# Forgetting attention pairs: the high halves of weight strips and of the output projection's row tiles made by ScalarE instead of GpSimd

## What is computed

```
h = x @ w_in                                    # q, k, v of both head groups, and the forget gates
cum = cumsum(log_sigmoid(f_logit))              # per forgetting head
logits = q.k * scale + cum_q - cum_k            # causal
ob = softmax(logits) @ v                        # forgetting heads
mixer = concatenate([oa, ob]) @ w_o             # one output projection
x = layer_norm(ALPHA * x + mixer)
```

## Time and profile before

| | |
|---|---|
| median of three runs | 2824.18 us |
| the profiled execution | 2827.21 us, its span 2825.40 us |
| TensorE busy | 2687.5 us, 95% of the span |
| VectorE busy | 1903.7 us, 67% |
| ScalarE busy | 1080.0 us, 38% |
| GpSimd busy | 1676.1 us, 59% |
| granted TensorE clock | 0.993 of full speed |
| the four forgetting pairs | from 296 to 509 us |

### The profile page before, as it was taken

The page is one execution under the profiler, slowest core; times in us unless marked ns, Lnnn a source line. Parts: engine busy times, 40 slices in busy tenths (PEclk is TensorE's granted clock), DMA queues, the critical chain, the costliest instruction groups (busy, mean ns, idle before and its releaser), DMA issues.

```text
span 2825.4 us, 42474 instructions
## 1 busy us (share of the span) xinstructions
PE 2687.5 (95%) x15813; PEld 1363.5 (48%) x16096; DVE 1903.7 (67%) x2637; ACT 1080.0 (38%) x1665; POOL 1676.1 (59%) x916
## 2 busy tenths in 40 slices
PE   7999898899999999999899999899999999999998
PEld 4666554354444444444444444456654444444443
DVE  6788778575666674256999999688847656664043
ACT  3566566243333210014554343666643433331000
POOL 4777656336676679845347777711113666675884
PEclk9999999999999999999999999999999999999999
DMA  4122455631111253332213222488873111113332
GB/s 150 50 64 72 90 119 119 193 115 60 58 53 55 68 179 127 105 132 83 53 38 142 111 79 100 114 183 185 185 208 132 68 60 60 60 54 126 127 105 97
DMA packets 299309, 294.82 MB, mean 104 GB/s; under 512 B 239408, under 2 KB 239536, under 8 KB 299168
## 3 DMA queue, kind: packets, MB, share of 16 engines
q1 hardware_dynamic: 287360, 268.90, 33.1%
q10 hardware_dynamic: 11808, 23.99, 2.6%
HBM read 189.51 MB, written 35.70 MB: 80 GB/s over the span
## 4 chain that ended last, share of the span: by engine, by line
PE 78%; DVE 6%; issue 5%; ACT 4%; DMA 4%; POOL 2%; ACTq 1%; POOLq 0%; DVEq 0%; SPq 0%
PE ps L1691 23%; PE ps L334 20%; PE ps L316 14%; PE ps L650 4%; PE ps L2529 4%; PE ps L399 4%; DMA pt<-split 3%; PE ps L920 2%; PE ps L2019 2%; PE ps L656 1%; PE ps L2063 1%; DVE split L848 1%; PE ps L2557 1%; PE ps L891 1%; DVE prob L1035 1%
## 5 line engine op out<-in xcount | busy, mean ns | idle before, releaser
L273 POOL TENSOR_TENSOR w_hi<-w_stage,ones 128x1024 bf16<-128x1024 f32 (+1 forms) x115 | 238.5, 2074 | 138.1 <-PE ps L334 85.3
L276 POOL TENSOR_TENSOR w_lo<-w_stage,w_hi 128x1024 bf16<-128x1024 f32 (+1 forms) x115 | 265.2, 2306 | 9.0
L1508 DVE SCALAR_TENSOR_TENSOR x_res<-x_res,ps 128x1024 f32<-128x1024 f32 x32 | 39.0, 1218 | 319.6 <-PE ps L334 318.8
L334 PE MATMUL ps<-w_hi,hid_hi 128*128 128x512 bf16 x689 | 206.4, 379 | 1.6 <-POOL w_lo L276 0.8
L334 PE MATMUL ps<-w_hi,hid_lo 128*128 128x512 bf16 x690 | 206.5, 379 | 0.7
L334 PE MATMUL ps<-w_lo,hid_hi 128*128 128x512 bf16 x690 | 206.4, 379 | 0.7
L2529 PE MATMUL ps<-lat_hi,q_now 128*128 128x512 bf16 (+3 forms) x736 | 185.9, 326 | 7.6 <-DVE row_max L2616 6.8
L316 PE MATMUL ps<-xt_hi,w_hi 128*128 128x512 bf16 x598 | 179.2, 380 | 3.1 <-DVE score L2178 2.5
L316 PE MATMUL ps<-xt_hi,w_lo 128*128 128x512 bf16 x596 | 179.0, 380 | 0.8 <-issue 0.2
L316 PE MATMUL ps<-xt_lo,w_hi 128*128 128x512 bf16 x592 | 178.1, 380 | 0.8
L1691 PE MATMUL ps<-xt_lo,w_hi 128*128 128x512 bf16 x426 | 161.5, 379 | 0.5
(11 more groups left out here) (309 smaller groups left out, 7507.6 us busy)
## 6 DMA issues: line engine op xcount, KB each, us to landing
w_stage<-in_l_up SPq DMA_DIRECT2D x88, 512.0 KB, 3.8
w_stage<-in_l_down SPq DMA_DIRECT2D x88, 512.0 KB, 3.7
w_stage<-in_l_o SPq DMA_DIRECT2D x32, 512.0 KB, 6.2
w_stage<-in_l_q SPq DMA_DIRECT2D x32, 512.0 KB, 5.1
q_split<-q_out SPq DMA_DIRECT2D x32, 512.0 KB, 2.6
q_now<-q_split SPq DMA_DIRECT2D x16, 1024.0 KB, 5.7
w_stage<-in_l_qkv SPq DMA_DIRECT2D x24, 512.0 KB, 4.1
x_spilled<-x_res ACTq DMA_DIRECT2D x16, 512.0 KB, 2.6
```

Of the source, the lines that this page charges most:

```text
L273: pool.tensor_tensor(hi, w_stage[slot][:, 0:cols], ones[:, 0:1].to_broadcast([P, cols]), ALU.mult).then_inc(w_cast[slot], 1)
L276: pool.tensor_tensor(lo, w_stage[slot][:, 0:cols], hi, ALU.subtract).then_inc(w_split[slot], 1)
L334: mm = pe.matmul(ps[:, bank + h, :], a[:, k, rows], w[:, h * HALF:(h + 1) * HALF], start=(k == first and m == 0), stop=(k == tiles - 1 and ...
```

## The change

In the forgetting pairs, GpSimd no longer makes high halves of weights. ScalarE makes them with a copy that rounds to bfloat16, at the end of a slot, after the exponential: strips 2, 0 and 1 in slots 2, 6 and 11, the row tiles 3, 0, 1 in slots 7, 8 and 12 of pair 6, and the row tiles 2, 4, 5, 6, 7 in slots 3, 4, 6, 9 and 11 of pair 7. The waits for the load and for the last use of the buffer go with the copy to ScalarE. GpSimd waits for the copy and subtracts. Its steps for the tiles of pair 7 move from 1, 3, 5, 7, 9 to 3, 4, 6, 9, 11. ScalarE's loop over pairs 5 and 6 is written out, since its slots now differ. Loads, SyncE's list, TensorE's and VectorE's lists are the same.

```diff
@@ -989,6 +989,7 @@
                     act.activation(take[t % 4][:, 0:n], banks(2 * (t % 2))[:, 0:n], ACT.Exp, scale=SB_SCALE,
                                    bias=neg_max[:, t % 4:t % 4 + 1],
                                    accum_out=row_sum[:, t % 4:t % 4 + 1]).then_inc(s_sfree, 1)
+                    fox_weights_hi(act, pair, slot)
 
         def pair_vector(dve, pair, kind, prev, project):
 
@@ -1048,6 +1049,29 @@
             pool.wait_ge(w_cast[n], feed_qkv.use(n, pair) + 1)
             pool.tensor_tensor(w_lo[n][:, :], w_stage[n][:, :], w_hi[n][:, :], ALU.subtract).then_inc(w_split[n], 1)
 
+        def fox_weights_hi(act, pair, slot):
+
+            qkv = {2: (2, pair + 1), 6: (0, pair + 2), 11: (1, pair + 2)}
+            outputs = {7: 3, 8: 0, 12: 1} if pair == N_PAIRS - 2 else {3: 2, 4: 4, 6: 5, 9: 6, 11: 7}
+            if slot in qkv and qkv[slot][1] < N_PAIRS:
+                n, of = qkv[slot]
+                act.wait_ge(w_loaded[n], 16 * (feed_qkv.use(n, of) + 1))
+                act.wait_ge(s_pj, 6 * (of - 1) + 2 * (n + 1))
+                act.activation(w_hi[n][:, :], w_stage[n][:, :], ACT.Copy).then_inc(w_cast[n], 1)
+            elif pair >= N_PAIRS - 2 and slot in outputs:
+                n = outputs[slot]
+                act.wait_ge(w_loaded[feed_o0.slot(n)], 16 * (feed_o0.use(n, 0) + 1))
+                if n != 3:
+                    act.wait_ge(s_pj, 6 * (N_PAIRS - 1) + 2 * (n + 1) if n < 2 else 6 * N_PAIRS)
+                act.activation(held(feed_o0, n)[0], w_stage[feed_o0.slot(n)][:, 0:D_MODEL],
+                               ACT.Copy).then_inc(w_cast[feed_o0.slot(n)], 1)
+
+        def output_lo(pool, n):
+            slot = feed_o0.slot(n)
+            hi, lo = held(feed_o0, n)
+            pool.wait_ge(w_cast[slot], feed_o0.use(n, 0) + 1)
+            pool.tensor_tensor(lo, w_stage[slot][:, 0:D_MODEL], hi, ALU.subtract).then_inc(w_split[slot], 1)
+
         def pair_gpsimd_sb(pool, pair):
             for t in range(STEPS):
                 n = (query_block(t) + 1) * P
@@ -1177,36 +1201,22 @@
 
             def splits_ahead(pair):
                 def splits(t):
-                    if t == 2:
-                        split_qkv_hi(pool, 2, pair + 1)
-                    elif t == 3:
+                    if t == 3:
                         split_qkv_lo(pool, 2, pair + 1)
-                    elif t in (6, 11):
-                        split_qkv_hi(pool, t // 11, pair + 2)
                     elif t in (7, 12):
                         split_qkv_lo(pool, t // 12, pair + 2)
                 return splits
 
             def splits_last(t):
-                if t == 2:
-                    split_qkv_hi(pool, 2, N_PAIRS - 1)
-                elif t == 3:
+                if t == 3:
                     split_qkv_lo(pool, 2, N_PAIRS - 1)
-                elif t == 7:
-                    split_piece(pool, feed_o0, 3, 0)
-                elif t == 8:
-                    pool.wait_ge(s_pj, 6 * (N_PAIRS - 1) + 2)
-                    split_piece(pool, feed_o0, 0, 0)
-                elif t == 12:
-                    pool.wait_ge(s_pj, 6 * (N_PAIRS - 1) + 4)
-                    split_piece(pool, feed_o0, 1, 0)
+                elif t in (7, 8, 12):
+                    output_lo(pool, {7: 3, 8: 0, 12: 1}[t])
 
             def splits_o(t):
-                if t == 1:
-                    pool.wait_ge(s_pj, 6 * N_PAIRS)
-                ahead = {1: 2, 3: 4, 5: 5, 7: 6, 9: 7}
+                ahead = {3: 2, 4: 4, 6: 5, 9: 6, 11: 7}
                 if t in ahead:
-                    split_piece(pool, feed_o0, ahead[t], 0)
+                    output_lo(pool, ahead[t])
 
             with pool.Fori(N_SB // 2, N_PAIRS - 2) as pair:
                 pair_gpsimd_fox(pool, pair, splits_ahead(pair))
@@ -1231,7 +1241,16 @@
             make_current_qk(act, 1, 0)
             for hh in range(2):
                 make_current_v(act, hh, 0)
-            all_pairs(act, pair_scalar)
+            first_fox = N_SB // 2
+            pair_scalar(act, 0, "sb", None, True)
+            with act.Fori(1, first_fox - 1) as pair:
+                pair_scalar(act, pair, "sb", "sb", True)
+            pair_scalar(act, first_fox - 1, "sb", "sb", True)
+            pair_scalar(act, first_fox, "fox", "sb", True)
+            for pair in range(first_fox + 1, N_PAIRS - 1):
+                pair_scalar(act, pair, "fox", "fox", True)
+            pair_scalar(act, N_PAIRS - 1, "fox", "fox", False)
+            pair_scalar(act, N_PAIRS, None, "fox", False)
 
         def heads_vector(dve):
             for e in range(4, 6):
```

## The result

The changed kernel takes 2830.2 us (median of 19 runs, 2826.6 to 2832.6), the kernel before 2825.2 in the runs beside them (19 runs, 2823.1 to 2827.4). The ratio is 1.0015 with a 95% interval from 1.0009 to 1.0021: slower by 0.15%, some 4 us by the ratio and 5.0 between the medians, which is under the 0.2% taken as the bound. The forecast was +4.5 us.

What follows compares the result with a forecast made beforehand. The loop of VectorE and ScalarE was taken to set the pace in the last forgetting pair, with some TensorE slack in middle pairs. Terms 0.3 + 1.0 + 0.3 - 1.25 + 4.15 = +4.5 us gave median 2828.7, range 2819 to 2837.

Steps and rivals of the forecast that it cites:

- pair 4: New block at slot 2 costs 0.2, slots 5 to 7 end 0.2 early, slot 11 is 0.5 late: +0.3 after rounding.
- pair 5: Blocked or delayed splits around slots 2, 5 to 7 and 11 make the pair 1.0 us longer.
- pair 6: First, tile 3's passes given back at slot 7: -0.7; second, tile 1's copy in slot 12 delays a high half: +1.0.
- pair 7, first half: Slots 2 to 7: slot 2's split is free; slots 4, 5 and 7 each meet a low half and copy; gain 1.25.
- pair 7, second half: Slots 9 and 11: ScalarE waits 2.7 and 3.1 us for the loads of tiles 6 and 7; pair end +4.15.
- Slot 2 of pair 5: Copy fits ScalarE's idle time; the low half from 363.8 blocks the 896-column split until 366.9: loss 0.8.
- Slots 5 to 7: Pair 5: 640-column split gains 1.25, the low half delays the 384-column split to 378.0; 0.5 late in all.
- Slot 11: Copy 0.3 late; the 768-column split starts 0.15 us ahead of GpSimd's low half, which makes the next split 0.5 late.
- the rival that lost it: Low half starts before slot 11's split, 1.6 lost in each of three pairs: +9.3, time 2833.5; chance 0.25.
- The end: TensorE's closing products start at 508.70 and go on without a gap for 80 us, carrying the delay in full.
- The signs: Trace signs: splits' total falls from 77 us by less than 8, slot 3's 896-column splits take 2 us; wrong if excess halves.
- The faster rival: Passes taken off GpSimd free the splits of slots 5 to 7 and pair 7: 7.3 less about 0.5, time 2817.5; chance 0.15.

Runs made afterwards that it cites:

- 3: The kernel before with only ScalarE's loop over pairs 5 and 6 written out: ratio 1.0003.
- 5: The kernel before with the loads of row tiles 6 and 7 moved earlier in SyncE's list: 2822.1 us, ratio 0.9989.
- 1: The changed kernel with the high halves of row tiles 6 and 7 back on GpSimd: ratio 1.0002 to the kernel before.
- 2: The changed kernel with the high halves of all strips back on GpSimd, row tiles still on ScalarE: ratio 1.0012 to the kernel before.
- 4: The changed kernel with the loads of row tiles 6 and 7 moved earlier in SyncE's list: 2823.0 us, ratio 0.9992 to the kernel before.
- 8: The changed kernel with tiles 6 and 7 loaded earlier, all strips and row tile 1 back on GpSimd: 2821.2 us, ratio 0.9986 to the kernel before.
- 6: The changed kernel with each low half also waiting for VectorE's split of the slot before its copy's: 2822.0 us, ratio 0.9993 to the kernel before.
- 7: The changed kernel with both early loads of tiles 6 and 7 and low halves waiting behind splits: 2820.4 us, ratio 0.9979 to the kernel before.
- 10: The kernel before with early loads of tiles 6 and 7, every high and low GpSimd pass waiting for a split: 2818.9 us, ratio 0.9970.
- 9: The changed kernel with early loads, low halves behind splits, and row tile 1's copy in slot 11 of pair 6: 2816.1 us, ratio 0.9962 to the kernel before.

## Why the prediction was right

The sum was right, and its parts nearly so, the waits for the loads above all. Against the starts of the splits:

```
                      predicted    trace
pair 4                   +0.3      +0.1
pair 5                   +1.0      +0.6
pair 6                   +0.3      +0.6
pair 7, first half       -1.25     -1.6
pair 7, second half      +4.15     +4.3
sum                      +4.5      +3.9
```

How firm a part is shows in the other profiles. Pair 7's first half takes 21.08 or 21.09 us before and in experiments 3 and 5, 19.46 after and in 1, 2, 4 and 8. Pair 6 takes 49.19 to 49.23 before, in 3 and in 5, 49.81 and 49.83 after and in 1. Pair 5 takes 53.82, 54.18 and 54.39 before, in 3 and in 5, and 54.36 to 54.42 after, in 1 and in 4: its +0.6 may be less, down to nothing. Pair 4 is the same within its spread.

*Slot 2 of pair 5.* Predicted: low half at 363.8, the 896-column split ends 0.8 later than before. Measured: low half at 363.60, the split ends at 366.68, 0.6 late. Experiment 6 freed exactly this split.

*Slots 5 to 7.* The 640-column split takes 0.87 (0.9 predicted), the 384-column one ends at 377.79 where 378.0 was predicted.

*Slot 11.* The race was won as forecast, by 0.27 us where I had 0.15; the rival that lost it stayed out. Its price was counted too high: I gave the race to three pairs, but only pairs 4 and 5 have a copy in slot 11, the third stands in slot 12 of pair 6.

*Pair 6.* The first term held: counted from the pair's first split, TensorE's product at slot 8 starts 0.8 us earlier (0.7 predicted). The second was short: from there to `nv_lo`'s product the changed kernel takes 1.4 us more, where 1.0 was predicted, 0.95 of it the longer wait behind row tile 1's copy. And a fall of the clock behind this wait (experiments 2, 4, 6, 7) had no term of its own. I had allowed 2 us for the clock and taken zero. That the profiled execution of the changed kernel had no spell there is luck: with one, pair 6 takes up to 1.6 us more.

*Pair 7.* The waits for the loads are 2.62 and 3.52 us, predicted 2.7 and 3.1. From the seventh split to the end of the ninth the changed kernel is 3.5 us later (3.7 predicted), to the end of the tenth 1.7 (2.0 predicted). The point that decided was to ask, for a wait moved from an idle engine to one in the loop, behind what its load is issued. Experiments 1 and 4 take 4.3 and 6.3 us out of pair 7 and the waits with them.

*The end.* I had said that the delay is carried to the end in full. The medians, 5.0 us apart, are in keeping with it; the two profiled executions, 2.6 apart in their spans, do not show it.

*The signs.* The splits' total was to fall by less than 8 us and fell by 8.7. The 896-column splits in slot 3 of pairs 5 and 6 take 1.83 us (2 predicted), and the excess did not halve (25 to 16).

*The faster rival* asked that the low halves fall between splits and the tiles be in time. Neither held in the changed kernel. Numbers 4 and 6 make them hold one by one and number 7 together, and then it is the right story: 2823.0, 2822.0 and 2820.4. The rule of the Trainium skill that spoke for it ("Perfetto Trace Analysis", section "Optimizing GPSIMD Operations": prefer other engines) is not borne out by the change itself, which is slower, and experiment 10 leaves it at most some 3 us once loads and timing are right. The other rule of the Trainium skill ("SBUF — State Buffer", section "Who interferes with whom": issue order decides who is blocked) is what experiments 6 and 10 turn into a gain, and 5 in part: no pass was made cheaper, only started at another time. The trace agrees: 1.83 us for 384 columns behind a low half, 0.62 beside none.

One step on the way fell. I had said of the old passes of tiles 6 and 7 that GpSimd could afford to wait for its loads. It could, but when the loads came, the passes hit two splits on the chain: number 5 shows 1.8 us of pair 7 to be had there.

What stays open: gains over the kernel before differ between median and marker, by 2.4 us in experiment 4, 2.3 in 5, 2.8 in 6 and 3.4 in 9, and the spread of the stretch behind the last split is of that size; and it is not known how often the low clock comes in each kernel, since one profile per kernel doesn't tell. A kernel with number 9's placement and GpSimd's high halves was not tried, so the worth of ScalarE's copies alone is open.

## What to carry to other kernels

Moving a pass to another engine also moves the moment at which its second half starts; look up what is due on a shared resource at that moment before counting the time taken off. A wait for a load that was harmless on an idle engine must be traced back to where the load is issued before it is put into the engine that paces the loop: here the issue stood behind work that waited for that same engine. And when two engines block each other, one added wait that starts the longer pass just behind the other's operation can give more than removing work: -4.6 us of the marker here, -6 by the ratios and -8 by the medians, for one semaphore wait per pass.

## What was not expected of the hardware

A 2.13 us pass of GpSimd started right behind a split left the next split at 1.04 us for 768 columns (1.02 free), although the gap between the two was 1.98 us and the pass ended 0.23 us inside the split; in a gap of 1.39 us it cost the next split 0.6 us (1.50 for 0.88). And TensorE's granted clock fell to 1.2 GHz for 3.4 us behind a wait of 2.27 or 2.28 us before `nv_lo`'s product in four of six profiles with it (2, 4, 6, 7, not the changed kernel and 1), and in none of the six with 1.32 to 1.48 us (before, 3, 5, 8, 9, 10). Where it did, pair 6 took 1.3 to 1.6 us more in the kernels with ScalarE's strips (51.08, 51.10 and 51.45 for 49.81 in the changed kernel). Two almost equal kernels differ by that much from one profile to the next.
